# Layer 1's conditioning columns formed on VectorE instead of TensorE in a two-layer transformer block

## The reference

```python
mx = jnp.split((silu_c @ ada_w[layer] + ada_b[layer])[:, None, :], N_MOD, axis=-1)
mc = jnp.split((silu_cc @ ada_w[layer] + ada_b[layer])[None, None, :], N_MOD, axis=-1)
...
hx = modulate(rms_norm(x, norm_g[layer, 0]), mx[0], mx[1])
hc = modulate(rms_norm(h_ctx, norm_g[layer, 0]), mc[0], mc[1])
zx = hx @ w_in[layer]
...
x = x + mx[2] * rms_norm(ox, norm_g[layer, 1])
...
fx = hier_moe(modulate(rms_norm(x, norm_g[layer, 2]), mx[3], mx[4]), ...)
x = x + mx[5] * rms_norm(fx, norm_g[layer, 3])
```

## Time and profile before

| | |
|---|---|
| median of 3 runs | 1154.69 us (1148.52 to 1158.79) |
| the profiled execution | 1154.22 us, span 1152.4 us |
| TensorE busy | 983.6 us, 85% of the span; mean granted clock 0.942 |
| VectorE, ScalarE, GpSimd busy | 313.6, 269.0, 189.3 us |
| input projections of layer 0 | 34 to 148 us |
| its mixer with the 17 ada items | 166 to 318 us |

### The profile page before, as it was taken

The page is one execution under the profiler, slowest core; times in us unless marked ns, Lnnn a source line. Parts: engine busy times, 40 slices in busy tenths (PEclk is TensorE's granted clock), DMA queues, the critical chain, the costliest instruction groups (busy, mean ns, idle before and its releaser), DMA issues. The chain is left out here.

```text
span 1152.4 us, 24721 instructions
## 1 busy us (share of the span) xinstructions
PE 983.6 (85%) x9692; PEld 601.4 (52%) x9693; DVE 313.6 (27%) x872; ACT 269.0 (23%) x714; POOL 189.3 (16%) x312
## 2 busy tenths in 40 slices
PE   3999999999999588887799818999999778898676
PEld 2354646565555455554566516676754445564343
DVE  2100045446633521111111132005472511111013
ACT  4121024444523110100011144103562110000002
POOL 0010015000004221111121120002401222222111
PEclk9999999999999789999999958999999799998888
DMA  9983527766454669899999975323113769999992
GB/s 376 360 263 109 219 104 266 288 238 238 160 204 186 255 246 417 348 422 425 408 354 381 411 271 178 139 73 146 75 38 114 291 256 406 427 429 428 428 428 84
DMA packets 56423, 313.67 MB, mean 272 GB/s; under 512 B 12282, under 2 KB 20516, under 8 KB 37796
## 3 DMA queue, kind: packets, MB, share of 16 engines
q1 hardware_dynamic: 36480, 280.00, 60.5%
q0 software_dynamic: 7152, 24.58, 6.1%
q10 hardware_dynamic: 12724, 8.14, 2.3%
HBM read 304.24 MB, written 14.75 MB: 277 GB/s over the span
## 5 line engine op out<-in xcount | busy, mean ns | idle before, releaser
L946 PE MATMUL psum<-weights,lat 128*32 128x256 f32 x2688 | 161.8, 393 | 40.5 <-DVE lat L1791 15.3
L946 PEld LDWEIGHTS psum<-weights,lat 128*32 128x32 f32 x2688 | 100.4, 113 | 96.5 <-issue 55.8
L549 PE MATMUL psum<-hT,weights 128*128 128x512 f32 (+1 forms) x336 | 120.7, 519 | 3.6 <-ACT lat L1141 2.1
L549 PEld LDWEIGHTS psum<-hT,weights 128*128 128x128 f32 x336 | 64.7, 194 | 57.3 <-issue 48.8
L969 PE MATMUL psum<-weights,lat 128*32 128x256 f32 x1344 | 82.8, 386 | 6.0 <-ACT lat L1313 6.0
L1304 ACT ACTIVATE lat<-psum 128x128 f32<-128x128 f32 x64 | 17.7, 277 | 288.1 <-PE psum L946 229.6
L1791 DVE TENSOR_TENSOR lat<-lat,psum 128x128 f32<-128x128 f32 x64 | 23.7, 371 | 205.2 <-ACT lat L1304 205.1
L1533 DVE TENSOR_REDUCE st<-psum 128x1 f32<-128x512 f32 (+1 forms) x96 | 55.8, 598 | 75.6 <-PE psum L685 26.2
L722 PE MATMUL psum<-weights,R 128*128 128x64 f32 x480 | 63.7, 272 | 5.5 <-ACT R L1219 4.1
L1206 ACT ACTIVATE R<-psum,st 128x512 f32<-128x512 f32 (+1 forms) x78 | 48.0, 616 | 87.1 <-DVE st L1533 43.3
L946 PE MATMUL psum<-hT,lat 128*32 128x256 f32 x672 | 45.7, 417 | 25.7 <-issue 14.3
(11 more groups left out here) (309 smaller groups left out, 1326.2 us busy)
## 6 DMA issues: line engine op xcount, KB each, us to landing
weights<-in_exp_w_gu_dram SPq DMA_DIRECT2D x44, 2048.0 KB, 13.4
weights<-in_ada_w_dram SPq DMA_DIRECT2D x24, 2048.0 KB, 7.4
weights<-in_exp_w_down_dram SPq DMA_DIRECT2D x22, 2048.0 KB, 15.1
hT<-in_exp_w_gu_dram SPq DMA_DIRECT2D x10, 2048.0 KB, 11.9
R<-in_exp_w_gu_dram SPq DMA_DIRECT2D x10, 2048.0 KB, 14.0
spare_w<-in_exp_w_down_dram SPq DMA_DIRECT2D x10, 2048.0 KB, 13.0
weights<-in_w_in_dram SPq DMA_DIRECT2D x6, 2048.0 KB, 12.4
weights<-in_w_out_dram SPq DMA_DIRECT2D x4, 2048.0 KB, 7.9
```

The lines of the kernel that those rows point to most:

```text
L549: mm = nc.tensor.matmul(t[:, lo:hi], w[:, k, col:col + P], hT[:, k, lo:hi], start=(k == 0), stop=(k == KD - 1))
L946: mm = nc.tensor.matmul(gu_ps[BLK * j:BLK * j + BLK, 0:256], (xgT if L < LAST else xgT_last)[:, k, :], w[:, k % 4, j, :, :], start=(k == 0 ...
```

## The change

Layer 1's ada items 4 to 11 (its second and third third of the columns) are taken from TensorE. `fold` on VectorE multiplies a staged item's rows by the latent stream's `silu_c`, one scalar per partition, and adds the eight k-tiles up in a 128 x 2048 accumulator for each third (`folds`, in `R1` and the head of `spare_w`): four instructions of 128 x 1024 per item, the first k-tile by `tensor_scalar`, the others by `scalar_tensor_tensor`. `fold_sum` on TensorE then sums the accumulator over its partitions by four matmuls with `ones`; ScalarE copies the result out, and `ada_turn` and `ada_columns` go on as before. All eight folds stand in VectorE's order behind `ident16` and ahead of `latents(0)`. `fold_sum` stands between `project(0)` and `latent_projections(0)`, the transposes behind the latter, the columns at i = 1 and 2 of the mixer.

The load order changes with it: the eight folded items come between the input chunks, all through slot 5; chunks use slots 3 and 4 in turn, ada items 4 to 6 slot 0. The nine remaining items lie in the mixer at i = 0, 5, 10, 14, 18, 21, 24, 33 and 42. GpSimd gets two waits, for `fold_sum` and for the transposes, ahead of its writes to `spare_w`.

```diff
--- before.py
+++ after.py
@@ -272,6 +272,9 @@
         o = NTOK + 4 * PADW
         sq = [part(spare_w, o + i * NTOK, NTOK) for i in range(2)]
         shift2_row = part(spare_w, o, 2 * NTOK)
+
+        folds = {1: [part(R1, 0, D), part(R1, D, D)], 2: [part(R1, 2 * D, D), part(spare_w, 0, D)]}
+        folded_sb = {1: sq[0], 2: sq[1]}
         rstd = part(spare_w, o + 2 * NTOK, NTOK)
         assert SPARE_ADA == o + 3 * NTOK
         ada_sb = part(spare_w, SPARE_ADA, NTOK)
@@ -418,9 +421,12 @@
                 ROPES[L][f"qa{i}"] = (qas[L][0:MLA_QK, i, 0:SEQ], "mla", 0, MLA_QK)
 
 
-        items = [("ada", 0, i) for i in range(4)] + [("in", 0, i) for i in range(3)]
-        items += [("ada", 0, 4), ("in", 0, 3)] + [("ada", 0, i) for i in range(5, 12)] + [("ada", 1, i) for i in range(12)]
-        items += [("out", 0, i) for i in range(2)]
+
+        FOLDED = [("ada", 1, i) for i in range(4, 12)]
+        items = [("ada", 0, i) for i in range(4)] + [("in", 0, 0), ("in", 0, 1), ("ada", 0, 4)] + FOLDED[0:3] + [("in", 0, 2), FOLDED[3], ("in", 0, 3)]
+        items += [FOLDED[4], ("ada", 0, 5)] + FOLDED[5:7] + [("ada", 0, 6), FOLDED[7]]
+        late_items = [("ada", 0, i) for i in range(7, 12)] + [("ada", 1, i) for i in range(4)] + [("out", 0, i) for i in range(2)]
+        items += late_items
         n_stage0 = len(items)
         items += [("in", 1, i) for i in range(4)] + [("out", 1, i) for i in range(2)]
         item_no = {it: n for n, it in enumerate(items)}
@@ -428,13 +434,16 @@
 
 
         first_buffers = {("ada", 0, 0): 0, ("ada", 0, 1): 1, ("ada", 0, 2): 2, ("ada", 0, 3): 5}
-        buffers, n = [], 0
+        buffers = []
         for it in items[:n_stage0]:
-            if it[:2] == ("ada", 0) and it[2] < 7:
+            if it in late_items:
+                buffers.append(3 + late_items.index(it) % 3)
+            elif it in FOLDED:
+                buffers.append(5)
+            elif it[0] == "in":
+                buffers.append(3 + it[2] % 2)
+            else:
                 buffers.append(first_buffers.get(it, 0))
-            else:
-                buffers.append(3 + n % 3)
-                n += 1
         buffers += [3 + n % 3 for n in range(len(items) - n_stage0)]
 
         def stage_source(it):
@@ -457,7 +466,10 @@
 
         def ada_plan(L):
 
-            return [it for it in items if it[0] == "ada" and it[1:] >= (0, 7)] if L == 0 else []
+            return [it for it in late_items if it[0] == "ada"] if L == 0 else []
+
+
+        ADA_STEPS = (0, 5, 10, 14, 18, 21, 24, 33, 42)
 
         block = ctx.enter_context(nc.Block())
 
@@ -520,9 +532,19 @@
 
                 pe.wait_ge(*at("ada_sb", L, r))
                 t = take("adaT", L, r)
+                src = folded_sb[r] if L and r else ada_sb
                 for q in range(4):
-                    mm = nc.tensor.transpose(t[:, q * P:(q + 1) * P], ada_sb[:, q * P:(q + 1) * P], ident)
+                    mm = nc.tensor.transpose(t[:, q * P:(q + 1) * P], src[:, q * P:(q + 1) * P], ident)
                 mm.then_inc(*mark(S, ("filled", "adaT", L, r)))
+
+            def fold_sum(r):
+
+                pe.wait_ge(*at("folded", r))
+                t = take("fold", r)
+                for g in range(4):
+                    mm = nc.tensor.matmul(t[32 * g:32 * g + 32, :], ones[:, 0:32], folds[r][g // 2][:, g % 2 * 512:g % 2 * 512 + 512],
+                                          start=True, stop=True, skip_group_check=True)
+                mm.then_inc(*mark("pe_fold", ("filled", "fold", r)))
 
             def project(L):
                 S, nq = f"pe_in{L}", q_tokens(L)
@@ -762,7 +784,7 @@
                             t = take("pool", L, j, banks=ring)
                             nc.tensor.matmul(t[:, 0:nq], w_pool[:, j, :], dgs[L][:, j, 0:nq], start=True, stop=True)\
                                 .then_inc(*mark(S, ("filled", "pool", L, j)))
-                    while done < len(ada) and done * len(U) <= i * len(ada):
+                    while done < len(ada) and ADA_STEPS[done] <= i:
                         ada_item(S, ada[done])
                         _, la, ia = ada[done]
                         done += 1
@@ -771,7 +793,7 @@
                     if i >= len(U):
                         if i == len(U):
                             if ada:
-                                ada_turn(S, 1, 2)
+                                ada_turn(S, 1, 0)
                             pe.wait_ge(*at("mixT_some", L))
                         if i < len(U) + 2:
                             out_some(L, 0, i - len(U), ring)
@@ -1058,7 +1080,13 @@
                     pe.wait_ge(*at("banks_out", L - 1))
                     turn_combined("pe_comb", L, 0)
                 project(L)
+                if L == 0:
+                    for r in (1, 2):
+                        fold_sum(r)
                 latent_projections(L)
+                if L == 0:
+                    for r in (1, 2):
+                        ada_turn("pe_fold", 1, r)
                 mix(L)
                 project_out(L)
                 route(L)
@@ -1430,6 +1458,9 @@
                 if L == 0:
                     rest_of_loads()
                 project(L)
+                if L == 0:
+                    for r in (1, 2):
+                        copy("act_fold", folded_sb[r], ("fold", r), keys=[("ada_sb", 1, r)])
                 latent_projections(L)
                 if L == 0:
                     act.wait_ge(*at("lam_dots"))
@@ -1475,6 +1506,24 @@
                 else:
                     tt_(amp[L][:, 3, :, :], mod[L][:, 40:48, :], gains(3), ALU.mult)
                     stt(amp[L][:, 2, :, :], mod[L][:, 32:40, :], 1.0, gains(2), ALU.add, ALU.mult).then_inc(*mark(S, ("amp", L, 2)))
+
+
+            def fold(S, i):
+
+                it = ("ada", 1, i)
+                r, kk = i // 4, i % 4
+                v.wait_ge(*at("staged", item_no[it]))
+                w = stage[buffers[item_no[it]]].rearrange("p (k h n) -> p k h n", k=2, h=2)
+                for k2 in range(2):
+                    k = 2 * kk + k2
+                    for half in range(2):
+                        if k == 0:
+                            ins = ts(folds[r][half], w[:, k2, half, :], silu_c[:, k, 0:1], None, ALU.mult)
+                        else:
+                            v.wait_ge(*at("fold", r, half, k - 1))
+                            ins = stt(folds[r][half], w[:, k2, half, :], silu_c[:, k, 0:1], folds[r][half], ALU.mult, ALU.add)
+                        last = k2 == 1 and half == 1
+                        ins.then_inc(*mark(S, ("fold", r, half, k), *([("used", item_no[it])] if last else []), *([("folded", r)] if last and kk == 3 else [])))
 
             roped = []
 
@@ -1588,8 +1637,10 @@
                             diff_norm(L, q)
                     if i in ROPED_LATE:
                         rope_late(S, L, ROPED_LATE[i])
-
-                    while done < len(ada) and done * len(U) <= (i - 1) * len(ada):
+                    if L == 0 and i in (1, 2):
+                        ada_columns("v_fold", 1, i)
+
+                    while done < len(ada) and ADA_STEPS[done] <= i - 1:
                         _, la, ia = ada[done]
                         if ia % 4 == 3:
                             ada_rows(S, la, ia // 4)
@@ -1598,7 +1649,7 @@
                         done += 1
                     if ada and i == len(U) + 1:
                         assert done == len(ada)
-                        ada_columns(S, 1, 2)
+                        ada_columns(S, 1, 0)
                 diff_norm(L, tiles(L) - 1)
 
             def diff_sums(L, q):
@@ -1918,6 +1969,9 @@
             v.wait_ge(*at("const"))
             nc.vector.tensor_copy(band[:, :], C("band"))
             nc.vector.tensor_copy(ident16[:, :], ident).then_inc(*mark("v_band", ("band",)))
+            v.wait_ge(*at("filled", "x0", KD - 1))
+            for _, _, i in FOLDED:
+                fold("v_fold", i)
             for L in range(DEPTH):
                 latents(L)
                 if L == 0:
@@ -1961,6 +2015,8 @@
                     step(gt(dst[r:, 0:ns, lo:hi], src[r:, 0:ns, lo - half:hi - half], src[r:, 0:ns, lo + half:hi + half], ALU.add))
 
                 g_.wait_ge(*at("read", f"u{j}", L))
+                if L == 0:
+                    g_.wait_ge(*at("filled", "fold", 2))
                 if j == 0:
                     g_.wait_ge(*at("x_cos", L, "dk1"))
                 step(gt(pa[:, 0:ns, 1:PADW], up[j][:, 0:ns, 0:PADW - 1], up[j][:, 0:ns, 1:PADW], ALU.add))
@@ -2009,6 +2065,8 @@
                 g_.wait_ge(*at("roped", L, "dk1"))
                 vector_row(L, ROW_GATE1, 0, gate1_row, "gate1_row")
                 g_.wait_ge(*at("sq_used", ("ckv", L), 0))
+                if L == 0:
+                    g_.wait_ge(*at("filled", "adaT", 1, 2))
                 vector_row(L, ROW_SHIFT2, 0, shift2_row, "shift2_row")
                 g_.wait_ge(*at("filled", "o", L, len(units(L)) - 1))
```

## The result

The change makes the kernel slower: 1187.53 us (median of 4 runs, 1186.43 to 1188.58) against 1154.66 us, a ratio of 1.0291, interval 1.0258 to 1.0323. The forecast was 1171 us in a range of 1157 to 1182: the direction was right, the size was outside the range. The ratios and intervals here and in the table of experiments leave out executions over 1.5% above the kernel's fastest (e8, e9, e10 and e14 have some); the medians include them. The profiled execution has a span of 1185.6 us, 33.2 us over that of before. The page has 37 us more on VectorE, as planned.

The account below looks back on a forecast made before the run. TensorE, busy for 85% of the span, was taken as the bound, with VectorE nearly full at the mixer's ends. Stall 23.8, fold_sum 1.9, clock 2 and mixer -10.7 gave +17.0 on 1154.2: 1171 us, range 1157 to 1182.

Parts of the forecast that it names:

- What bounds, and the wait: TensorE bounds projections and mid-mixer; late folds delay cqn, ScalarE's Ln and evictions, stopping TensorE at u0 for 23.8 us.
- The last fold, taken at 154.7: VectorE's eighth fold ahead of latents(0) ends at 154.7 us, the middle between 148.3 and 161.
- equal sharing: Folded loads and GpSimd's zeroing split the DMA engines equally; a load's transfer takes 10 us, last fold at 161.
- the undisturbed end: The last fold ends at 148.3 us if the zeroing and the folded loads don't delay each other.
- the estimate of 154: With packet-by-packet turns, loads keep over two thirds of the DMA engines; last fold at about 154 us.
- `fold_sum` 1.9: Two sums of four strip matmuls each, added on TensorE around the projections: 1.9 us.
- clock behind the stall 2: After TensorE's idle stretch ahead of u0, work at 1.2 instead of 2.4 GHz costs 2 us, between 0 and 3.5.
- "Covered" chunks: Input chunks 2 and 3, loaded later, land near 86 and 98 us, before TensorE wants them at 91.26 and 120.67.
- The mixer, -10.7: Eight removed ada items give 14.8 us, less 2.8 at the mixer's ends and 1.3 for added columns: 10.7.
- The sum: Whole kernel: stall 23.8, fold_sum 1.9, clock 2, mixer -10.7, together +17.0 us.
- Rival (b): Bigger loss: stall 30.1 ahead of u0, fold_sum 1.9, clock 3.5, mixer -9, together +26.5, 1181 us; chance 0.16.
- Later stages take up nothing: After the mixer, no anchor in absolute time takes up a shift; mixer's end to last instruction changes by at most a few us.

Follow-up runs that it names:

- e8: Changed kernel with folded items loaded as 1 MB halves, GpSimd's zeroing after the last fold, last two ada items at i = 30 and 40: 1145.24 to 1180.73 us.
- e9: Changed kernel, whole loads, cq scaled behind the first fold and ckv behind the third, zeroing after the last fold, last ada items at 30 and 40: 1148.36 us.
- e10: e8 with VectorE's scaling of cq put behind the second half load and that of ckv behind the sixth: 1152.63 us, ratio 0.9964.
- e14: e13 with the last two ada items back at i = 33 and 42, as in the changed kernel: 1159.80 us, ratio 1.0024.
- e1: Changed kernel with VectorE's scaling of cq behind the first fold and of ckv behind the third, instead of behind all eight: 1163.99 us, ratio 1.0055.
- e2: Changed kernel with GpSimd's zeroing of y_rows started only after the last fold: 1178.15 us, ratio 1.0185.
- e13: e9 with VectorE's scaling of cq behind the second fold instead of the first: 1148.91 us, ratio 0.9954.
- e5: Changed kernel with its last two ada items in the mixer moved from i = 33 and 42 to 30 and 40: 1174.34 us, ratio 1.0152.
- the twins: e13 and e14, which differ only in the places of the last two ada items: 1148.91 and 1159.80 us.
- e4: Kernel before, its 17 ada items in the mixer moved to other steps, none between i = 24 and 33, nothing removed: 1170.46 us, ratio 1.0131.
- e11: Kernel before with 32 matmuls of 512 columns added in the mixer at u = 28, 31, 37 and 40, overwritten by the scores: 1158.48 us.
- e6: Changed kernel with 32 matmuls of 512 columns on real operands added at u = 28, 31, 37 and 40, overwritten by the scores: 1245.36 us, one run.

## Why the prediction was right and wrong

- **What bounds, and the wait:** right. The named chain (fold, `cqn`, `Ln` L1125, evictions, `u0`) is in the trace link by link, and e1 removed it.
- **The last fold, taken at 154.7:** it ended at 160.65, the upper bound that equal sharing gave. An undisturbed turn was well worked out (12.6 against 12.2 us), and so was the undisturbed end (148.3; with the zeroing late, e2 has 150.6 and e13 149.0). What was too small was the delay by the zeroing: 6.4 us taken for want of a row, 10 measured by e2 and 11.7 by e13. With it the stall was 28.3 instead of 23.8. That equal sharing gave the right end is luck, for the engines were not shared equally. By the Trainium skill (DMA: Bandwidth & Descriptors, "Queues, rings and completion order") each DMA engine takes turns between its queues packet by packet. The trace agrees: 207 packets against 208, and 1.70 against 0.85 MB, from 118 to 124 us. What went wrong in the estimate of 154 that the prediction drew from this rule is the length of the zeroing. With a third of the engines it took 35.9 us, until 137, instead of 24.2, and so met the seventh load too, which was issued at 130.5 and landed after 12.9 us instead of 7.4. Why that load lost 5.5 us to the zeroing's last 7 us isn't shown.
- **`fold_sum` 1.9 and clock behind the stall 2:** measured 1.7 and 1.9.
- **"Covered" chunks:** right. TensorE waited for none; the 0.9 us ahead of chunk 2 come from the clock in chunk 0.
- **The mixer, -10.7: this step failed.** It came to -0.1. The count of the work was not too high: at full clock the mixer shrank by 165 - 151 = 14 us, so hardly an item stood uselessly. But I priced the clock only behind the stall, and took it for granted in the mixer because the windows of before had 1.00 there. Taking eight items out of TensorE's stream and placing the rest elsewhere brought 27 us more at 1.2 GHz, worth 13.5 us. e5, which moves two items and nothing else, takes 14 us off the mixer, and the twins and e4 point the same way. So the placing cost the time; the loss of the eight items by itself did not (e5 has no more items than after).
- **The sum:** 4.5 (stall) + 0.9 + 10.6 (mixer) + 0.3 (rest) is 16.3 us, but for rounding the distance from +17.0 to +33.2. With the mixer's term right the time would have lain near 1177, inside the range. Rival (b) came close to the stall (30.1 against 28.3), by an equal sharing that didn't happen, and still missed, since it too let the mixer give 9.
- **"Later stages take up nothing":** right, +0.3.

What activity TensorE needs to keep 2.4 GHz stays open. Items at i = 30 and 40 kept it in e5 but for 3 us, equal amounts at u = 28, 31, 37 and 40 kept it in the kernel before (e11) and not in the changed one (e6).

## What to carry on

Work moved to an idle engine is free only if nothing already on that engine's queue is waited for: put the old instructions between the new ones, which took 19.7 us off the first stage in e1 (183.2 to 163.5). Work taken off TensorE also takes away activity, so look at the granted clock where it was, and place what is left to keep it. And a term for two transfers side by side needs the length of both: the one with the smaller share lasts longer, and meets loads that would have come behind it.

## What was unexpected of the hardware

- TensorE ran at 1.2 GHz for 17 us while busy without a gap (window 280 to 300 of after), and got its clock back at a dense item.
- Two kernels with 32 matmuls more in the mixer lost 49 us in another layer's experts, in waits put down to issue, with 28 more packets of instructions; 16 more, or 32 in the kernel before, cost nothing there.
- With the zeroing's 6 MB in flight, two loads of 2 MB took 12.4 and 12.9 us to land instead of 7.4, and the zeroing's two transfers 24.8 and 35.9 us instead of 16.2 and 24.2. Packets went one for one (207 and 208), bytes two for one.
